# Computing one gate projection between the steps of stick-breaking attention

## The reference

```python
h = rms_norm(x, norm_gain[layer])
proj = jnp.einsum('bsd,dc->bsc', h, w_in[layer])
(sb_q, sb_k, sb_v, sb_g, r_q, r_k, r_v, r_g, m_sb, m_ret) = jnp.split(proj, SPLIT_POINTS, axis=-1)
...
out_a = merge_heads(stick_breaking_attention(qa, ka, va)) * jax.nn.silu(sb_g)      # 8 heads of 128
...
out_b = merge_heads(ret) * jax.nn.silu(r_g)                                        # retention, 4 heads of 256
p_a = jnp.einsum('bsw,wd->bsd', out_a, w_branch_sb[layer])
p_b = jnp.einsum('bsw,wd->bsd', out_b, w_branch_ret[layer])
merged = (jax.nn.sigmoid(m_sb + b_merge[layer, 0]) * p_a
          + jax.nn.sigmoid(m_ret + b_merge[layer, 1]) * p_b)
x = x + jnp.einsum('bsd,de->bse', merged, w_out[layer])
```

## Time and profile before

| | |
|---|---|
| median of 3 runs | 3065.61 us (3042.84 to 3065.85) |
| span of the profiled execution | 3050.2 us (its time beyond the span is not given) |
| TensorE busy | 2875.8 us, 94% |
| TensorE weight load busy | 2394.9 us, 79% |
| VectorE busy | 1092.1 us, 36% |
| ScalarE busy | 881.6 us, 29% |
| mean granted clock of TensorE | 0.971 |

### The profile page before, as it was taken

How to read it: one execution, slowest core, us unless ns; L and a number is a source line. 1 busy time by engine, 2 the same in 40 slices (tenths; PEclk the granted TensorE clock), 3 DMA queues, 4 the chain that set the end, 5 groups by cost and what they waited for, 6 DMA issues and landing times.

```text
span 3050.2 us, 37125 instructions
## 1 busy us (share of the span) xinstructions
PE 2875.8 (94%) x15762; PEld 2394.9 (79%) x15762; DVE 1092.1 (36%) x1288; ACT 881.6 (29%) x1332; POOL 50.3 (2%) x78
## 2 busy tenths in 40 slices
PE   6889797979999999999999999998899999999998
PEld 5767575757887878778899767786698998979888
DVE  3342516254122313323234383356425323232232
ACT  4453535354211210113223142233314112021122
POOL 0000000000000000000011000000010000000000
PEclk9999999999999999999999998897799999999999
DMA  2001010101121111102123100000021111111112
GB/s 105 28 14 41 14 41 0 41 14 51 66 88 43 41 34 41 34 28 97 55 95 125 42 1 28 28 29 14 16 97 48 42 44 54 42 50 48 42 44 88
DMA packets 111830, 141.66 MB, mean 46 GB/s; under 512 B 3021, under 2 KB 103546, under 8 KB 111594
## 3 DMA queue, kind: packets, MB, share of 16 engines
q1 hardware_dynamic: 104714, 112.29, 11.2%
q0 software_dynamic: 7008, 27.77, 2.5%
HBM read 127.46 MB, written 12.58 MB: 46 GB/s over the span
## 4 chain that ended last, share of the span: by engine, by line
PE 88%; DVE 4%; ACT 3%; issue 2%; DVEq 2%; ACTq 1%; POOL 0%; DMA 0%; POOLq 0%
PE ps L443 42%; PE ps L437 25%; PE ps L1420 2%; PE ps L1485 2%; PE ps L1474 2%; PE ps L1720 2%; PE ps L1395 2%; PE ps L1653 2%; DVEq L1015 1%; PE ps L1735 1%; PE ps L1434 1%; PE ps L1533 1%; DVE l L984 1%; ACT l L674 1%; PE ps L1379 1%
## 5 line engine op out<-in xcount | busy, mean ns | idle before, releaser
L443 PE MATMUL ps<-a_hi,w_hi 128*128 128x512 f32 x1568 | 636.2, 406 | 13.8 <-DMA causal<-tab_causal 6.3
L443 PE MATMUL ps<-a_lo,w_hi 128*128 128x512 f32 x1568 | 624.6, 398 | 0.0
L443 PE MATMUL ps<-a_hi,w_lo 128*128 128x512 f32 x1568 | 620.2, 396 | 0.0
L418 ACT ACTIVATE w_hi<-w_raw 128x2048 fp32r<-128x2048 f32 x98 | 187.5, 1914 | 862.0 <-DMA w_raw<-in_w_ff 364.9
L422 DVE TENSOR_TENSOR w_lo<-w_raw,w_hi 128x2048 fp32r<-128x2048 f32 x98 | 224.4, 2291 | 549.0 <-ACT w_hi L418 537.8
L443 PEld LDWEIGHTS ps<-a_hi,w_hi 128*128 128x128 f32 x1568 | 297.2, 190 | 93.5 <-issue 16.5
L443 PEld LDWEIGHTS ps<-a_lo,w_hi 128*128 128x128 f32 x1568 | 296.8, 189 | 75.4 <-issue 8.6
L443 PEld LDWEIGHTS ps<-a_hi,w_lo 128*128 128x128 f32 x1568 | 297.7, 190 | 67.6
L437 PE MATMUL ps<-w_hi,a_hi 128*128 128x256 f32 x1152 | 328.6, 285 | 5.1 <-DVE a_lo L1262 5.1
L437 PE MATMUL ps<-w_lo,a_hi 128*128 128x256 f32 x1152 | 325.9, 283 | 0.0
L437 PE MATMUL ps<-w_hi,a_lo 128*128 128x256 f32 x1152 | 325.9, 283 | 0.0
(11 more groups left out here) (280 smaller groups left out, 3669.1 us busy)
## 6 DMA issues: line engine op xcount, KB each, us to landing
w_raw<-in_w_in SPq DMA_DIRECT2D x50, 1024.0 KB, 5.0
w_raw<-in_w_ff SPq DMA_DIRECT2D x32, 1024.0 KB, 5.4
w_raw<-in_w_out SPq DMA_DIRECT2D x8, 1024.0 KB, 5.1
xt<-in_x SPq DMA_DIRECT2D x8, 512.0 KB, 5.8
w_raw<-in_w_branch_sb SPq DMA_DIRECT2D x4, 1024.0 KB, 5.3
gated_pa<-stage POOLq DMA_DIRECT2D x16, 256.0 KB, 2.3
w_raw<-in_w_branch_ret SPq DMA_DIRECT2D x4, 1024.0 KB, 5.1
out_t<-gated_pa POOLq DMA_DIRECT2D x1, 4096.0 KB, 12.5
```

What stands on the lines that cost most here:

```text
L418: act.activation(W_hi[s][:, :, :], W_raw[s][:, :, :], ACT.Copy).then_inc(w_hi, 1)
L443: last = pe.matmul(bank[banks[j]][:, :], w[s][:, k, ct * P:(ct + 1) * P], a[:, k, t0 + th * HALF:t0 + (th + 1) * HALF], start=(k == 0 and ...
```

## The change

The gate projection of the first merge branch (m_sb, four blocks) is computed in the attention pairs, one block in each, after the pair's own gate block. A pair so has five blocks: Q, K, V, its gate, and a merge gate block. As five is odd, the slots swap from pair to pair, and the loop over four pairs becomes a loop over two with two pairs in it. The filler on TensorE is 192 matmuls a pair in eight outputs, with the last steps given in FILL_ENDS, and the order within a step is: scores of S + 2, half of the filler, turn, weigh, the rest of the filler. Outputs 4 to 7 go through `stage` (moved into attention's memory) to HBM in raw form, by POOL. In the first merge branch there are two gate blocks of the second branch (m_ret, first half; stored raw as well) and then the four branch blocks in a row. The gates come back from HBM into NB and pass the sigmoid there. The second branch has gate, branch, gate, branch, branch, branch; the gates of its last two are those stored before. Weights of n + 4 and n + 5 are split in steps 4 and 13 on both ScalarE and VectorE.

The diff, cut to its core:

```diff
         PASSES = 3 * KT
-        gate_upto = [PASSES + -(-PASSES * S // 5) for S in range(2 * TT)]
-        gate_ends = {gate_upto.index(PASSES * (j + 1)): j for j in range(4)}
+        FILL_ENDS = (0, 2, 4, 6, 8, 11, 13, 15)
+        fill_upto, fill_after = [], {}
+        for J, end in enumerate(FILL_ENDS):
+            first = len(fill_upto)
+            fill_upto += [PASSES * J + PASSES * (S - first + 1) // (end - first + 1) for S in range(first, end + 1)]
+            fill_after[end] = J
...
-        L1, B1, L3, B2, L5 = 0, 16, 24, 40, 48
+        L1, B1, L3, B2, L5 = 0, 20, 26, 42, 48
...
# SyncE
+            for s in range(2):
+                load_block(sp, B1 + s, s, w1_d[:, :, 9, (2 + s) * BC:(3 + s) * BC])
+            for b in range(4):
+                load_block(sp, B1 + 2 + b, b % 2, wbs_d[:, :, b * BC:(b + 1) * BC])
...
# POOL
                 for j in range(4):
                     th, ct = j // 2, j % 2
-                    pool.wait_ge(kept[j], kept_by(B1 + 2 * i + 1))
-                    pool.dma_start(pa_d[:, ds(2 * i + ct, 1), th * HALF:(th + 1) * HALF].rearrange("p a b -> p (a b)"),
+                    pool.wait_ge(g_raw, 8 * i + (5 + j))
+                    pool.dma_start(ms_d[:, ds(2 * i + ct, 1), th * HALF:(th + 1) * HALF].rearrange("p a b -> p (a b)"),
                                    stage[j % 2][:, :]).then_inc(pa_stored[j % 2], 16)
...
+            def gate_again(src, k, j):
+                th, ct = j // 2, j % 2
+                pool.dma_start(NB[j][:, :], src[:, k + ct, th * HALF:(th + 1) * HALF]).then_inc(mg_in[j], 16)
...
+            for b in range(4):
+                for j in range(4):
+                    th, ct = j // 2, j % 2
+                    pool.wait_ge(kept[j], kept_by(B1 + 2 + b))
+                    pool.dma_start(pa_d[:, 2 * b + ct, th * HALF:(th + 1) * HALF], stage[j % 2][:, :]).then_inc(pa_stored[j % 2], 16)
+                    if b < 3:
+                        gate_again(ms_d, 2 * b + 2, j)
...
# ScalarE, in a pair
                     if S < 14:
                         softplus_terms(S + 2, S)
                     else:
                         keep_first(S)
-                    if S == 7:
-                        split_hi(act, n + 4, 0)
-                keep_gate(3)
+                    if S == 4:
+                        split_hi(act, n + 4, u % 2)
+                    if S == 13:
+                        split_hi(act, n + 5, (u + 1) % 2)
+                keep_filler(7)
...
# ScalarE, first and second branch
+            for i in range(4):
+                if i:
+                    gate_from_store(0, i, i + 1)
+                if i < 3:
+                    split_hi(act, B1 + 4 + i, i % 2)
...
+            split_hi(act, B2 + 5, 1)
+            merged_hi(0)
+            gate_from_store(1, 2, 5)
+            merged_hi(1)
+            split_hi(act, L5, 0)
+            gate_from_store(1, 3, 6)
+            merged_hi(2)
...
# VectorE, in a pair
                     if S < 14:
                         clamp(S + 2)
-                    if S == 8:
-                        split_lo(dve, n + 4, 0)
+                    if S == 4:
+                        split_lo(dve, n + 4, u % 2)
+                    if S == 13:
+                        split_lo(dve, n + 5, (u + 1) % 2)
...
# VectorE, first branch
+            branch_low(0)
+            for s in range(3):
+                split_lo(dve, B1 + 1 + s, (1 + s) % 2)
+            for i in range(4):
+                n = B1 + 2 + i
+                if i < 3:
+                    split_lo(dve, n + 2, i % 2)
+                for j in range(4):
+                    dve.wait_ge(gp_done, done(n, j))
+                    dve.wait_ge(mg_sig, 4 * i + j + 1)
+                    dve.wait_ge(pa_stored[j % 2], 16 * (12 + 2 * i + j // 2))
+                    dve.tensor_tensor(stage[j % 2][:, :], bank[j], NB[j][:, :], ALU.mult).then_inc(kept[j], 1)
...
# VectorE, second branch
+            for i in range(4):
+                n = B2 + (1, 3, 4, 5)[i]
+                if i == 1:
+                    split_lo(dve, B2 + 5, 1)
+                if i >= 2:
+                    for k in range(2 * i - 4, 2 * i - 2):
+                        merged_lo(k + 1, k, slice(0, SEQ))
+                if i == 2:
+                    split_lo(dve, L5, 0)
...
+                for j in range(4):
...
+                    dve.tensor_tensor(NB[j][:, :], bank[j], NB[j][:, :], ALU.mult)
+                    dve.drain()
+                    dve.tensor_tensor(dst, dst, NB[j][:, :], ALU.add).then_inc(kept[j], 1)
...
# TensorE, in a pair
                 for S in range(16):
-                    if S - 1 in pair_after:
-                        weigh(pair_after[S - 1])
-                    if S < 14:
-                        scores(S + 2)
-                    if S == 0:
-                        gate_part(S)
-                    turn(S)
-                    if S:
-                        gate_part(S)
+                    first, upto = fill_upto[S - 1] if S else 0, fill_upto[S]
+                    early = first if S - 1 in fill_after else upto if S == 0 else (first + upto) // 2
+                    if S < 14:
+                        scores(S + 2)
+                    filler(first, early)
+                    turn(S)
+                    if S - 1 in pair_after:
+                        weigh(pair_after[S - 1])
+                    filler(early, upto)
                 weigh(7)
...
# TensorE, first branch
+            gemm(pe, B1, 0, A_hi, A_lo, False)
+            gemm(pe, B1 + 1, 1, A_hi, A_lo, False)
+            pe.wait_ge(s_lo[0], KT)
+            for b in range(4):
+                gemm(pe, B1 + 2 + b, b % 2, S_hi, S_lo, False)
...
# TensorE, second branch
+            gemm(pe, B2, 0, A_hi, A_lo, False)
+            pe.wait_ge(s_lo[1], KT)
+            gemm(pe, B2 + 1, 1, S_hi, S_lo, False)
+            gemm(pe, B2 + 2, 0, A_hi, A_lo, False)
+            for b in range(3):
+                gemm(pe, B2 + 3 + b, (1 + b) % 2, S_hi, S_lo, False)
```

More of the change, by code:

```diff
@@ L121, in build @@
     causal = work("causal", [P, P])
+    stage = [work(f"stage{u}", [P, HALF]) for u in range(2)]
     pos[0] = work_at
@@ L474, in build @@
         pa_back = sem("pa_back")
+        stage_free = sem("gate_staging_free")
+        mg_in, mg_sig = [sem(f"merge_gate{j}_in") for j in range(4)], sem("merge_gate_sigmoid")
         rtab, dec_in, rot_ok = sem("rotary_tables_in"), sem("decay_in"), sem("rotated")
@@ L529, in _ @@
                 sp.dma_start(XT[t - 4][:, :], x_d[t * P:(t + 1) * P, :]).then_inc(x_in[t - 4], 16)
-            for s in range(2, 4):
-                load_block(sp, L1 + s, s % 2, w1_d[:, :, s, 0:BC])
-            with sp.Fori(1, 4) as i:
-                for s in range(4):
[L534 to L545, removed]
+            for s, sec in ((2, 2), (3, 3), (4, 8)):
+                load_block(sp, L1 + s, s % 2, w1_d[:, :, sec, 0:BC])
@@ new lines, in _ @@
+            for b in range(4):
+                load_block(sp, B1 + 2 + b, b % 2, wbs_d[:, :, b * BC:(b + 1) * BC])
+            with sp.Fori(0, 4) as i:
+                for s in range(4):
+                    load_block(sp, L3 + 4 * i + s, s % 2, w1_d[:, :, 4 + s, ds(i * BC, BC)])
+            wbr_d = w_branch_ret[0].rearrange("(k p) c -> p k c", p=P)
+            for b in range(2):
+                load_block(sp, B2 + 2 * b, 0, w1_d[:, :, 9, b * BC:(b + 1) * BC])
+                load_block(sp, B2 + 2 * b + 1, 1, wbr_d[:, :, b * BC:(b + 1) * BC])
@@ L546, in _ @@
+            for b in range(2, 4):
+                load_block(sp, B2 + 2 + b, b % 2, wbr_d[:, :, b * BC:(b + 1) * BC])
             wo_d = w_out[0].rearrange("(k p) c -> p k c", p=P)
@@ L711, in _, with branch_low @@
                 act.preload_act_table_set(LOG_EXP)
-            def branch(b, B):
-                if b == 0:
-                    act.wait_ge(gated, 4 * 4 + 4)
+            with act.Fori(0, 2) as ii:
+                for u in range(2):
+                    sb_pair(2 * ii + u, L1 + 10 * ii + 5 * u, u)
+            def branch_low(b, B):
                 for j in range(4):
@@ L719, in branch, with merge_bias, gate_from_store @@
                     act.activation(S_hi[:, k, :], OUT[:, k, :], ACT.Copy).then_inc(s_hi[b], 1)
[L720 to L729, removed]
+                act.preload_act_table_set("sigmoid_and_others")
+            def merge_bias(b, i, j):
+                c = COLS["merge"] + 8 * b + 2 * i + j % 2
+                return cols[:, c:c + 1]
+            def gate_from_store(b, i, v):
+                for j in range(4):
+                    act.wait_ge(mg_in[j], 16 * v)
+                    act.activation(NB[j][:, :], NB[j][:, :], ACT.Sigmoid, bias=merge_bias(b, i, j)).then_inc(mg_sig, 1)
+            act.wait_ge(gated, 4 * 4 + 4)
+            branch_low(0, B1)
+            split_hi(act, B1 + 1, 1)
+            gate_from_store(0, 0, 1)
+            for s in range(2):
+                for j in range(4):
```

(18 more changed lines are left out.)

137 lines of the change are left out of this document (93 added, 44 removed).

## The result

The changed kernel takes 3095.81 us (median of 4 runs, 3091.27 to 3098.27). The kernel before, with one run more than the three above, has a median of 3057.16 us (3042.84 to 3065.85). The ratio is 1.0126, 95% interval [1.0082, 1.017]: slower, by 1.3%. The forecast was 3103.0 us and 1.2%.

The account below looks back on a forecast made before the run. TensorE, 94% busy, was taken as the bound, so time could only be won in its gaps. -89.0 + 56 + 52.4 + 12.0 + 6.0 = +37.4 us on a 3050.2 us span, plus 15.4 carried, gave 3103.0 us; range 3050 to 3135.

Parts of the forecast that it names:

- The work taken away, -89.0: Merge branches: four gate blocks leave the first branch, at 22.26 us each, saving 89.0 us.
- The merge gaps, +52.4: Merge branches: TensorE waits for VectorE's product behind a weight split, three times 10.2 and twice 10.9 us.
- Their clock, +12.0: Behind the five merge gaps TensorE's clock falls to half rate for a while, 2.4 us charged each.
- (e): Rival: the clock does not fall in the new gaps; +19 us, 3085 us, chance 0.07.
- Attention, +56 and +6.0 of clock: Four attention pairs: each grows 14 us as filler leaves gaps open, plus 1.5 us of slow clock behind its 7 us gap.
- three things said to push back: Attention: VectorE's copy ahead of the subtraction; split halves meeting at step 4 (2.75 us idle); likewise step 13 (7 us gap).
- the gain that I granted the new order: Attention: weighing behind the transposes removes waits for ScalarE's copy; step 6's scores come 3 us earlier.
- The 15.4 us that I carried from span to time: Whole kernel: the runs' median stood 15.4 us above the profiled span, unexplained, and was added to the forecast.
- (a): Rival: attention absorbs the gate, each pair growing 2 or 3 us; -15 us, 3051 us, chance 0.17.
- (b): Rival: the merge branch waits are absent because the release was misread; -27 us, 3039 us, chance 0.06.
- (c): Rival: both (a) and (b) hold; about -79 us, 2987 us, chance 0.03.
- (d): Rival: attention takes the gate with no gap filled, 22 us a pair; +69 us, 3135 us, chance 0.17.

Follow-up runs that it names:

- branch_order: Changed kernel with VectorE multiplying block n's outputs before splitting block n + 2's weights in both merge branches; 3027.09 us, ratio 0.99.
- split_stagger: Changed kernel with ScalarE's half of each weight split one step earlier, in steps 3 and 12; 3066.75 us, ratio 1.0025.
- unroll_tensor: Changed kernel with the loop over double pairs written out on TensorE's queue alone; 3086.42 us, measured once.
- copy_after_subtraction: Changed kernel with VectorE's copy of the attended values moved behind the subtraction of its step; 3085.28 us, ratio 1.0089.
- step_order_only: Kernel before with only the new order of TensorE's work in a step, without the additional filler; 3050.86 us, ratio 0.9996.
- four_mended: Changed kernel with merge products before splits, ScalarE's first split in step 3, second split in steps 9/10, TensorE loop written out, copy behind subtraction; 2963.15 us, ratio 0.968.

## Why the prediction was right

**The work taken away, -89.0.** Right. In branch_order the two branches take 263.7 us together where the kernel before took 352.8: 89.1 less for four blocks less.

**The merge gaps, +52.4.** Measured 51.8, at the five places named, 9.65 to 10.13 us and 10.67 and 11.41 us long. branch_order shows the cause: the same instructions in another order of VectorE's queue. The edits elsewhere leave these gaps as they are (51.9 to 52.5 us in split_stagger, unroll_tensor and copy_after_subtraction).

**Their clock, +12.0.** Measured 10.6, as the difference of stage times and waits. Rival (e), no fall of the clock, is refuted. The Trainium skill's rule on recurring waits ("HAM oscillation" in TensorE: Matmul & The Clock Gate) agrees with the trace: 0.64 and 0.59 behind gaps of 9.89 and 9.65 us, each time anew.

**Attention, +56 and +6.0 of clock.** Measured +68.3. The first and the fourth pair, without a loop's jump near them, grew by 13.6 us each; the second and third, around the jump, by 23.5 and 17.6. The places of the gaps were right, and the sizes within 0.4 us: 0.35 for 0.4, 2.48 for 2.75, 0.82 and 0.89 for 1.95 together, 6.63 for 7. A term was missing, the jump: 6.5 us of gap beyond the usual 0.76, and about 2.6 us of half rate behind it (a granted clock of 0.54 for 5.66 us). Without it (unroll_tensor) attention grew by 57.8 us, 4.2 less than the 62.0 of the two terms. Of the three things said to push back, the split at step 13 weighed most, then the one at step 4. The copy ahead of the subtraction was the least, worth about 9 us in all by its own run. The prediction named it first but rightly called the split at step 13 the worst; its expectation alone called it the first. And the gain that I granted the new order (waits for ScalarE's copy gone, scores of step 6 earlier) brings no time of its own, as step_order_only shows.

**The sum.** In spans, 3096.7 - 3050.2 = 46.5 us against 37.4 predicted. Attention was 6.3 us over its terms (the jump +10.5, the rest -4.2), the merge branches 2.1 under theirs, and 4.7 us lie in the unchanged rest. The 15.4 us that I carried from span to time were wrong: a run's time is 1.6 us above its span (3098.27 for 3096.7). They were the spread of the kernel before from run to run, 23 us wide in its four runs here and 30 us in the 24 later ones. The two errors partly cancelled, and the forecast stood 7 us off. That it came so near in microseconds is luck in part. The way and the mechanism are not: the five gaps and the five waits in a pair were named beforehand.

**The rivals.** (a), that attention takes the gate almost free, is false for this kernel, and true for the one with mended queues (6.8 us for four pairs). The Trainium skill's advice to interleave stages bound by different engines (Perfetto Trace Analysis, "Optimization Strategy") is then borne out: 6.8 us for 89.0 in four_mended. As written, the change lost all of that gain and more, mostly in the order of its queues. (b) and (c) are refuted by the five gaps. (d) is refuted by pairs 13.6 us longer, not 22; the second, at 23.5, has the jump in it.

## What to carry to other kernels

When blocks of work are regrouped, list for each in-order queue what each item waits for and who waits behind it. Here the weights of block n + 2 could not come before block n had ended, so their split may not stand ahead of the outputs of block n. Put the two halves of a hand-over (ScalarE's and VectorE's part of a split) at least a step apart, and away from the steps whose chain is longest. A gap costs its length and often the half rate behind it (about 2 us behind each gap of 10 to 11 us here), so repair the gaps before the change is given up: the idea cost 1.3% as written and gives 3.2% with the queues mended and TensorE's loop written out.

## What was not expected of the hardware

TensorE's jump back over a loop body of two pairs (some 1,650 matmuls) cost 6.63 us in which nothing is seen to be waited for; with the same instructions written out the gap was 0.76 us. The loop over one pair (some 730 matmuls) in the kernel before shows no such gap, and no instruction packet moves through its last three rounds.
